# Two of four activation buffers are shifted by 16 and 48 bytes against the 64-byte lines of SBUF

## The chip, the cores and the metric

The kernel runs on one core of a Trainium2 chip. The metric is the device time of one execution in microseconds.

## What is computed

Two transformer blocks one after the other, on 512 tokens of width 1024, in fp32. The first: a mixer (an eight-head forgetting attention and a gated linear attention beside it), a cross-attention over 256 memory tokens, and an MLP of width 4096 with a squared ReLU. The second: a gated MLP of width 2816, a token mixer (a differential attention, and a sparse attention with compressed, selected and windowed keys, merged by two gates), another gated MLP, and a last norm. Nearly all the work is dense products of activations with weight matrices:

```
proj = xn @ w_in
u = jax.nn.relu(rms_norm(h, norm_mlp_g) @ mlp_w1)
h = h + (u * u) @ mlp_w2
return (jax.nn.silu(h @ w1) * (h @ w3)) @ w2
merged = jax.nn.sigmoid(g_a) * (y_da @ w_proj_da) + jax.nn.sigmoid(g_b) * (y_ns @ w_proj_nsa)
```

## The kernel before, in words

A product of two fp32 matrices is made of three matmuls of the type float32r. Each operand is held as a high part and a low part (the high part is a rounded copy, the low part is the operand less the high part), and the helper `product` (L973 to L977) multiplies high by high (L975), high by low (L976) and low by high (L977) into the same PSUM bank. This is called a triple below. The second argument of a matmul in the code is the weights operand (loaded into the array), the third is the moving one (streamed through it); a profile's row names both, in no fixed order.

The activations lie in SBUF in two pairs of buffers, `xh` and `xl` (the pair X) and `ah` and `al` (the pair Y), each of 8 tiles of 128 partitions by 512 tokens, 16,384 bytes a partition. While one stage's input is read from one pair, the next stage's is often written into the other. The weights come as panels of 256 columns into `raw` (SyncE issues these DMAs), ScalarE makes the high part `wh` of a panel and VectorE the low part `wl`, each double buffered.

Four kinds of stage use these buffers:

- `panel_t` (L983): a panel's columns are the weights operand, 128 at a time, and the activations move, 512 columns wide. 2 x 8 triples a panel. This is most of L975 to L977.
- `panel_n` (L998): the activations are the weights operand and the panel's 256 columns move. Used where tokens are to lie on partitions.
- The MLPs' products by a Strassen-like scheme of seven products of half-size blocks (L1530 to L1532 and L1550 to L1552), 256 columns wide. Their operands are blocks of `arena_r`, `wh`, `wl` and, in some of them, of the X and Y buffers.
- Small products of the attentions, out of `arena`.

In the MLP stages the storage of the X and Y buffers that is not in use also takes raw weight blocks: `xh_f`, `xl_f`, `ah_f` and `al_f` are fp32 views of the same bytes as four blocks of 4 x 256 elements, written by DMA and read by ScalarE and VectorE. The low parts are written by VectorE: by a subtraction in `low` (L2817) and by one scalar-tensor-tensor operation (L2830) in `norm_low`.

The buffers are laid out one after another by an allocator that rounds to 32 bytes (L379 to L392). By the built program's addresses `h` begins at byte 2176 of a partition, `xh` at 18560, `xl` at 34944, `ah` at 51328, `al` at 67712, `raw` at 84096, `wh` at 100480, `wl` at 116864 and `cst` at 133248. All of these are multiples of 64. `arena` and `arena_r`, the same bytes, begin 32 bytes past a multiple of 64; blocks in them lie whole multiples of 64 bytes further. Tiles and blocks of the activation buffers, too, are whole multiples of 64 bytes long.

The order of work is written out by hand: each engine has its own list of instructions, with semaphores for what it needs of the others. The change touches no such list.

Of the kernel before, what the change touches and what calls it, by code (L numbers as in the profile page):

```python
# [7 lines left out]
F32 = mybir.dt.float32  # L8
F32R = mybir.dt.float32r
AX = mybir.AxisListType  # L10

PART = 128
T, M, D = 512, 256, 1024
KT = D // PART
PC = 256
QT = T // PART
HALF = 64
D_FF, D_FF2 = 4096, 2816
CMP_L, CMP_S = 32, 16
NCMP = (T - CMP_L) // CMP_S + 1  # L20
# [87 lines left out]
HT = KT // 2  # L108
# [198 lines left out]
def constants():  # L307
# [4 lines left out]
    def put(name, a):  # L312
        nonlocal at
        a = np.asarray(a, np.float32).reshape(PART, -1)
        where[name] = at
        at += a.shape[1]
        parts.append(a)
# [13 lines left out]
    put("cmpany", (valid.any(-1)).astype(np.float32).T)  # L331
    put("tril", (p[:, None] % HALF) <= np.arange(HALF)[None, :])
    put("chunk", np.tile(np.arange(T)[None, :] % HALF != 0, (PART, 1)))
    put("block", (p[:, None] // HALF) == (p[None, :] // HALF))
    inv = (np.float32(1.0) / (np.float32(10000.0) ** (np.arange(0, HALF, 2, dtype=np.float32) / np.float32(HALF)))).astype(np.float32)
    ang = (np.arange(T, dtype=np.float32)[:, None] * inv[None, :]).astype(np.float32)
    put("cos", np.cos(ang).T[p % (HALF // 2)])
    put("sin", np.sin(ang).T[p % (HALF // 2)] * np.where(p % HALF < HALF // 2, -1.0, 1.0)[:, None])
    sel = np.zeros((PART, 4))
# [29 lines left out]
def build(nc, d, out):  # L369
    ctx = ExitStack()  # L370
    with ctx:
        def sb(name, shape, dt=F32):
            return ctx.enter_context(nc.sbuf_tensor(name, shape, dt))
# [7 lines left out]
        xh = sb("xh", [PART, KT, T], F32R)  # L381
        xh_f = nc.alloc_sbuf_tensor_at("xh_f", [PART, 4, HT, PC], F32, offset=xh_at)
        xl_at = -(-nc.sbuf_base // 32) * 32
        xl = sb("xl", [PART, KT, T], F32R)
        xl_f = nc.alloc_sbuf_tensor_at("xl_f", [PART, 4, HT, PC], F32, offset=xl_at)
        ah_at = -(-nc.sbuf_base // 32) * 32
        ah = sb("ah", [PART, KT, T], F32R)
        ah_f = nc.alloc_sbuf_tensor_at("ah_f", [PART, 4, HT, PC], F32, offset=ah_at)
        al_at = -(-nc.sbuf_base // 32) * 32
        al = sb("al", [PART, KT, T], F32R)  # L390
        al_f = nc.alloc_sbuf_tensor_at("al_f", [PART, 4, HT, PC], F32, offset=al_at)
        raw = sb("raw", [PART, 2, KT, PC])  # L392
        wh = sb("wh", [PART, 2, KT, PC], F32R)
        wl = sb("wl", [PART, 2, KT, PC], F32R)
# [3653 lines left out]
```

## Time and profile before

| | |
|---|---|
| median of 3 runs | 2123.26 us (2122.52 to 2123.94) |
| the profiled execution's own time | 2123.62 us |
| its span, first to last instruction | 2121.8 us |
| TensorE busy, matmuls | 2103.8 us (99%), 13292 |
| TensorE busy, weight loads | 1816.3 us (86%) |
| VectorE busy | 1399.6 us (66%) |
| ScalarE busy | 1053.1 us (50%) |
| GpSimd busy | 52.0 us (2%) |

The matmuls overlap: one begins while the one before is still draining, so that the duration of a matmul in a row (390 ns for 512 columns) is longer than the distance from its start to the next one's start. That distance is read from a window, as its length by the number of matmuls that start in it, or from a timeline's column of starts.

### The profile page before, as it was taken

Reading aid. Unit: us, or ns where it says so; the run is one execution under the profiler, and the core shown is the slowest. Engines: PE = TensorE matmul, PEld = TensorE weight load, DVE = VectorE, ACT = ScalarE, POOL = GpSimd, SP = SyncE. Lnnn points to the kernel's source line nnn. Section 1 sums busy time; section 2 is a strip of 40 time slices with the busy share of each in tenths; the row PEclk is TensorE's granted clock in tenths of the full one; section 3 lists DMA queues with packets and bytes.
Section 4 is the critical chain, followed back from the end, with each engine's and each line's share of the span. In section 5 each row is a group of like instructions: output and inputs, shape, how many; then the busy total and the mean of one; then the engine's idle time right before and its main releaser. Section 6 shows DMA issues by size and latency. Waiting matters only on the chain.

```text
span 2121.8 us, 33199 instructions
## 1 busy us (share of the span) xinstructions
PE 2103.8 (99%) x13292; PEld 1816.3 (86%) x13292; DVE 1399.6 (66%) x2337; ACT 1053.1 (50%) x1762; POOL 52.0 (2%) x68
## 2 busy tenths in 40 slices
PE   9999999999999999999999999999999999999999
PEld 7888988888998988899988888887777888899997
DVE  4664663467665767688856777647776357678874
ACT  6664545443533543464543565546667234445454
POOL 0000000000000011110100000000000000000000
PEclk9999999999999999999999999999999999999999
DMA  5121522156355366875543522321111233345432
GB/s 191 60 81 61 192 94 72 40 149 189 102 167 145 94 160 173 229 204 159 142 137 102 179 85 81 99 85 51 27 50 33 88 99 95 104 126 154 129 91 79
DMA packets 210827, 243.83 MB, mean 115 GB/s; under 512 B 9953, under 2 KB 193394, under 8 KB 210162
## 3 DMA queue, kind: packets, MB, share of 16 engines
q1 hardware_dynamic: 199410, 208.15, 31.1%
q0 software_dynamic: 11264, 33.56, 7.4%
q8 instruction: 106, 1.74, 0.3%
q14 instruction: 47, 0.39, 0.1%
HBM read 232.77 MB, written 35.65 MB: 127 GB/s over the span
## 4 chain that ended last, share of the span: by engine, by line
PE 95%; DVE 2%; ACT 1%; issue 1%; DMA 0%; SPq 0%; DVEq 0%; ACTq 0%
PE lin L975 19%; PE lin L977 19%; PE lin L976 19%; PE turned L1076 3%; PE score L1171 3%; PE score L1551 3%; PE score L1552 3%; PE mix L1552 3%; PE mix L1551 3%; PE score L1550 3%; PE mix L1550 3%; PE mix L1185 2%; PE turned L1552 1%; PE turned L1551 1%; PE turned L1550 1%; PE mix L1724 1%
## 5 line engine op out<-in xcount | busy, mean ns | idle before, releaser
L975 PE MATMUL lin<-xh,wh 128*128 128x512 f32 (+1 forms) x968 | 382.5, 395 | 1.7 <-DVE wl L2812 1.2
L977 PE MATMUL lin<-xh,wl 128*128 128x512 f32 (+1 forms) x968 | 369.9, 382 | 0.0
L976 PE MATMUL lin<-xl,wh 128*128 128x512 f32 (+1 forms) x968 | 368.8, 381 | 0.0
L975 PE MATMUL lin<-ah,wh 128*128 128x512 f32 x724 | 283.6, 392 | 1.4 <-DVE al L2817 0.6
L977 PE MATMUL lin<-ah,wl 128*128 128x512 f32 x724 | 281.1, 388 | 0.0
L976 PE MATMUL lin<-al,wh 128*128 128x512 f32 x724 | 280.9, 388 | 0.0
L2806 DVE TENSOR_TENSOR wl<-raw,wh 128x2048 fp32r<-128x2048 f32 x77 | 176.5, 2293 | 117.8 <-ACT wh L1890 117.8
L975 PEld LDWEIGHTS lin<-xh,wh 128*128 128x128 f32 x968 | 182.2, 188 | 43.0 <-issue 9.6
L977 PEld LDWEIGHTS lin<-xh,wl 128*128 128x128 f32 x968 | 182.0, 188 | 36.3
L976 PEld LDWEIGHTS lin<-xl,wh 128*128 128x128 f32 x968 | 182.5, 188 | 32.5 <-issue 1.0
L1890 ACT ACTIVATE wh<-raw 128x2048 fp32r<-128x2048 f32 x77 | 146.8, 1906 | 95.9 <-PE lin L977 80.7
L975 PEld LDWEIGHTS lin<-ah,wh 128*128 128x128 f32 x724 | 136.0, 188 | 30.8 <-issue 1.6
L977 PEld LDWEIGHTS lin<-ah,wl 128*128 128x128 f32 x724 | 135.9, 188 | 28.1
L976 PEld LDWEIGHTS lin<-al,wh 128*128 128x128 f32 x724 | 136.0, 188 | 27.7 <-issue 0.2
L2812 DVE TENSOR_TENSOR wl<-raw,wh 128x1024 fp32r<-128x1024 f32 x90 | 109.5, 1221 | 40.2 <-ACT wh L1897 39.6
L2920 DVE CUSTOM_DVE_ANT_0 arena<-score,cst 128x128 f32<-128x128 f32 (+2 forms) x224 | 97.6, 487 | 57.7 <-PE score L1171 46.6
L1975 ACT ACTIVATE arena<-turned 128x512 f32<-128x512 f32 (+1 forms) x128 | 68.9, 582 | 112.4 <-PE turned L1076 112.1
L1987 ACT ACTIVATE arena<-arena,negm 128x128 f32<-128x128 f32 (+2 forms) x224 | 122.9, 555 | 3.0 <-DVE negm L2920 3.0
L2817 DVE TENSOR_TENSOR wl<-raw,wh 128x1024 fp32r<-128x1024 f32 x84 | 102.3, 1221 | 26.5 <-ACT wh L2435 25.2
L1897 ACT ACTIVATE wh<-raw 128x1024 fp32r<-128x1024 f32 x90 | 94.1, 1053 | 35.5 <-PE lin L977 22.2
L2435 ACT ACTIVATE wh<-raw 128x1024 fp32r<-128x1024 f32 x70 | 73.9, 1056 | 66.6 <-PE score L1552 22.0
L1551 PE MATMUL mix<-arena_r,wh 128*128 128x256 f32 x320 | 89.5, 280 | 0.0
(563 smaller groups left out, 4735.9 us busy)
## 6 DMA issues: line engine op xcount, KB each, us to landing
raw<-in_w_in_dram SPq DMA_DIRECT2D x38, 1024.0 KB, 5.3
raw<-in_ffn_w_dram SPq DMA_DIRECT2D x46, 512.0 KB, 4.3
raw<-in_mlp_w_dram SPq DMA_DIRECT2D x20, 1024.0 KB, 5.6
raw<-in_ffn_w_dram SPq DMA_DIRECT2D x20, 1024.0 KB, 5.3
up_sums_ffn<-in_ffn_w_dram POOLq DMA_DIRECT2D x32, 512.0 KB, 5.4
down_sums_ffn<-in_ffn_w_dram POOLq DMA_DIRECT2D x24, 512.0 KB, 5.9
raw<-in_xattn_wkv_dram SPq DMA_DIRECT2D x8, 1024.0 KB, 5.3
raw<-in_w_out_dram SPq DMA_DIRECT2D x8, 1024.0 KB, 5.2
```

The source lines that it names most:

```text
L975: nc.tensor.matmul(o, w[0], x[0], start=first, stop=False)
L976: nc.tensor.matmul(o, w[0], x[1], start=False, stop=False)
L977: return nc.tensor.matmul(o, w[1], x[0], start=False, stop=last)
L1550: nc.tensor.matmul(o[:, c, :], left_h[:, k, cols], right_h[:, k, :], start=begins, stop=False, skip_group_check=True)
L1551: nc.tensor.matmul(o[:, c, :], left_h[:, k, cols], right_l[:, k, :], start=False, stop=False, skip_group_check=True)
L1552: mm = nc.tensor.matmul(o[:, c, :], left_l[:, k, cols], right_h[:, k, :], start=False, stop=k == HT - 1, skip_group_check=True)
L1890: nc.scalar.activation(wh[:, p % 2], raw[:, p % 2], ACT.Copy).then_inc(hi_done, 1)
L1987: op = nc.scalar.activation(PB[:, s % 2, a, col:col + nk], SM[:, a, col:col + nk], ACT.Exp, bias=negm[:, at:at + 1], scale=-1.0, accum_out ...
L2806: nc.vector.tensor_tensor(wl[:, p % 2], raw[:, p % 2], wh[:, p % 2].bitcast(F32), ALU.subtract).then_inc(conv_done, 1)
L2812: nc.vector.tensor_tensor(wl[:, p % 2, :, cols], raw[:, p % 2, :, cols], wh[:, p % 2, :, cols].bitcast(F32), ALU.subtract).then_inc(conv_d ...
L2817: nc.vector.tensor_tensor(dst, full, hi.bitcast(F32), ALU.subtract).then_inc(done, 1)
L2920: op = nc.vector.tensor_tensor_reduce(out=SM[:, a, col:col + nk], in0=ps[a][:, col:col + nk], in1=mask, scale=scale, scalar=BIG, op0=ALU.a ...
```

## The change

`xl` and `al` each get an allocation longer by 16 elements (64 bytes), and begin 4 elements (16 bytes) and 12 elements (48 bytes) into it. Their fp32 views are made in the same way over the same bytes. With this `xl` begins at 34960 (16 past a multiple of 64), `ah` at 51392, `al` at 67824 (48 past), and all that follows lies 128 bytes further than before. No instruction is added, removed or moved, and none changes but for its addresses.

```diff
+LOW_X, LOW_Y = 4, 12
...
-        xl = sb("xl", [PART, KT, T], F32R)
-        xl_f = nc.alloc_sbuf_tensor_at("xl_f", [PART, 4, HT, PC], F32, offset=xl_at)
+        xl_room = sb("xl", [PART, 16 + KT * T], F32R)
+        xl = xl_room[:, LOW_X:LOW_X + KT * T].rearrange("p (k n) -> p k n", k=KT)
+        xl_f = nc.alloc_sbuf_tensor_at("xl_f", [PART, 16 + KT * T], F32, offset=xl_at)[:, LOW_X:LOW_X + KT * T].rearrange("p (b k n) -> p b k n", b=4, k=HT)
...
-        al = sb("al", [PART, KT, T], F32R)
-        al_f = nc.alloc_sbuf_tensor_at("al_f", [PART, 4, HT, PC], F32, offset=al_at)
+        al_room = sb("al", [PART, 16 + KT * T], F32R)
+        al = al_room[:, LOW_Y:LOW_Y + KT * T].rearrange("p (k n) -> p k n", k=KT)
+        al_f = nc.alloc_sbuf_tensor_at("al_f", [PART, 16 + KT * T], F32, offset=al_at)[:, LOW_Y:LOW_Y + KT * T].rearrange("p (b k n) -> p b k n", b=4, k=HT)
```

## Rows read from the trace of the kernel before

**Rows 1.** Spans by core, and of the page: busy times, and the chain's shares.

```profile
core 0: 2121.8 us, clock 1.000
...
PE 2103.8 (99%) x13292; PEld 1816.3 (86%) x13292; DVE 1399.6 (66%) x2337; ACT 1053.1 (50%) x1762; POOL 52.0 (2%) x68
...
PE 95%; DVE 2%; ACT 1%; issue 1%; DMA 0%; SPq 0%; DVEq 0%; ACTq 0%
```

**Rows 2.** Groups by form, TensorE: matmuls with a low part; busy us, mean ns.

```profile
L976 PE MATMUL lin<-xl,wh 128*128 128x512 f32 x888 | 346.2, 390 | 0.0
...
L976 PE MATMUL lin<-al,wh 128*128 128x512 f32 x716 | 278.7, 389 | 0.0
...
L977 PE MATMUL lin<-wh,xl 128*128 128x256 f32 x256 | 72.3, 283 | 0.0
...
L976 PE MATMUL lin<-xl,wh 128*128 128x256 f32 x80 | 22.6, 283 | 0.0
...
L1551 PE MATMUL score<-al,wh 128*128 128x256 f32 x48 | 13.6, 283 | 0.0
L1551 PE MATMUL score<-xl,wh 128*128 128x256 f32 x48 | 13.6, 283 | 0.0
...
L977 PE MATMUL lin<-wh,xl 128*128 128x512 f32 x32 | 12.4, 389 | 0.0
...
L1551 PE MATMUL mix<-xl,wh 128*128 128x256 f32 x32 | 9.1, 283 | 0.0
L1551 PE MATMUL mix<-al,wh 128*128 128x256 f32 x32 | 9.1, 283 | 0.0
```

**Rows 3.** Windows, TensorE: stretch, us, PE busy (matmuls), clock, DMA share, GB/s.

```profile
653.26:696.80 43.54, 43.54 (x194) 1.00 0.69 198
...
552.74:564.13 11.39, 11.39 (x98) 1.00 0.01 2
967.30:978.81 11.51, 11.51 (x98) 1.00 0.79 256
981.69:993.19 11.50, 11.50 (x98) 1.00 0.34 99
882.37:893.63 11.26, 11.26 (x98) 1.00 0.86 246
924.79:936.05 11.26, 11.26 (x98) 1.00 0.62 148
893.64:896.50 2.86, 2.86 (x26) 1.00 0.72 222
978.82:981.68 2.86, 2.86 (x26) 1.00 0.12 41
```

**Rows 4.** Timeline, TensorE, 512-wide matmuls after a break: start us, us.

```profile
280.49 0.40 PE L976 MATMUL lin<-al,wh 128*128 128x512 f32 x1
280.72 0.40 PE L977 MATMUL lin<-ah,wl 128*128 128x512 f32 x1
...
282.34 0.39 PE L975 MATMUL lin<-ah,wh 128*128 128x512 f32 x1
```

**Rows 5.** Groups by form, VectorE, line 2817; transfers: KB each, us to landing.

```profile
L2817 DVE TENSOR_TENSOR al<-arena,ah 128x512 fp32r<-128x512 f32 x54 | 36.8, 688 | 22.2 <-ACT ah L2371 10.7 <-ACT ah L2495 8.9 <-ACT ah L2444 1.4
...
L2817 DVE TENSOR_TENSOR arena_r<-arena,arena_r 128x512 fp32r<-128x512 f32 x20 | 13.3, 685 | 0.0
...
xl_f<-in_mlp_w_dram SPq DMA_DIRECT2D x12, 512.0 KB, 8.5
...
xl_f<-in_ffn_w_dram SPq DMA_DIRECT2D x6, 512.0 KB, 4.3
```

**Rows 6.** Waits of TensorE, the two longest: us in total, times, longest.

```profile
PE lin L1232 <- DMA gT<-in_gains_dram: 2.6, 1, 2.6
PE turned L1076 <- DVE arena L2936: 1.9, 4, 0.6
```

## The prediction

> **What bounds the kernel now.** I read the page first. TensorE is busy for 2103.8 of 2121.8 us, the granted clock is 1.000 of the 2.4 GHz level from end to end, and 95% of the chain that ended last is TensorE's own work [rows 1]. Its longest wait in the whole span is 2.6 us, before the first matmul; the next is 1.9 us in four pieces [rows 6]. So what counts is the distance from the start of one matmul to the start of the next, and the change can act on that alone: it adds, removes and moves no instruction.
>
> Next I read by form which matmuls touch the low parts [rows 2]. 512 columns wide: 888 with `xl` and 716 with `al` as the moving operand and 32 with `xl` as the weights, 1636 in all. 256 columns wide: 80, 48, 48, 32 and 32 with a low part moving, 256 with `xl` as the weights, and by the program's operands 112 more in smaller groups, 608 in all. Each is one of a triple (high by high, high by low, low by high), so 2244 triples hold one touched matmul, and the two others keep their addresses. Some 40 more have 48 or 64 weight columns; I leave them out.
>
> Then I took windows of uninterrupted matmuls, to read a distance with its addresses [rows 3]. A window counts also the two matmuls in flight at its edges, so 98 stand for 96 starts. By the program's addresses all buffers up to `cst` start on a 64-byte line and `arena` starts 32 bytes past one. I call that offset the phase of an operand.
> - 512 wide, `ah` and `al` with `wh` and `wl`, moving and weights at phase 0 (653.26): 43.54 us / 192 = 226.8 ns.
> - 256 wide, the X and Y buffers with `wh` and `wl`, both at 0 (967.30 and 981.69): 11.51 / 96 = 119.9 ns and 11.50 / 96 = 119.8 ns.
> - 256 wide, `arena_r` with `arena_r`, both at 32 (893.64): 2.86 / 24 = 119.2 ns.
> - 256 wide, `arena_r` moving at 32, weights `wh` and `wl` at 0 (882.37, 924.79): 11.26 / 96 = 117.3 ns; in another stage (552.74) 11.39 / 96 = 118.6 ns.
> - 256 wide, `ah` and `al` moving at 0, weights `arena_r` at 32 (978.82): 2.86 / 24 = 119.2 ns.
>
> So the phase matters in the kernel as it stands: equal phases give 120 ns steadily, unequal ones mostly less, never more. The last thing read is what a 512-wide run does after a break [rows 4]: from 280.49 to 282.34 it makes eight steps in 1.85 us, 231.3 ns each, uneven ones of 0.22 to 0.24 us, and then goes at an even 0.23. The even pace of 226.8 ns is thus something that the stream falls into, and it is the better pace for 512 columns, while for 256 columns the even pace (120) is the worse one. Whether the shifted operand keeps the stream out of that pace is the whole question.
>
> **The change part by part.**
> *High parts, weights, arena.* `ah` moves by 64 bytes and all behind `al` by 128, whole lines: their phases stay, priced at nothing.
>
> *Writers of the low parts.* DVE writes `al` at phase 0 in 688 ns and `arena_r` at phase 32 in 685 ns with the same operation and shape [rows 5], so a shifted output costs nothing; were it 10 ns on each of the some 250 operations, that would be 2.5 us on an engine busy for 66%, beside TensorE, whose largest wait for DVE is 1.9 us in four pieces [rows 6]. Nothing, then.
>
> *Transfers into the low parts.* By the program 21 land in `xl_f` and 9 in `al_f`, 512 KB each, in runs of 1 KB; the two largest groups, 12 and 6 of them, take 8.5 and 4.3 us [rows 5]. With a 16- or 48-byte offset a run touches one more 64-byte line, 17 for 16, an estimated 6% or 0.5 us of 8.5. No matmul waits for these transfers [rows 6], so I price it at nothing; were each of the 30 late by 0.5 us and nothing in between, 15 us would be the bound, and the cover is that SyncE runs buffers ahead.
>
> *Matmuls with a low part.* No row shows a 512-wide matmul at unequal phases. The nearest rows bound it. Below: the 117.3 ns of the unequal 256-wide run against 119.9, a gain of 2.6 ns. Taken for all three of a triple it is 7.8 ns x 2244 = 17.5 us. Above: the uneven pace, 231.3 against 226.8, a loss of 4.5 ns, taken for all three of the 1636 wide triples: 22.1 us. I take one gain of 2.6 ns in each triple, for the one matmul whose phase then differs from its partner's. The row is the nearest in kind (equal against unequal phases in an uninterrupted stream, same data type, same weights), and the loss belongs to a stream just restarted. Wide: 1636 x 2.6 ns = 4.3 us; narrow: 608 x 2.6 ns = 1.6 us. Sum: -5.9 us against the profiled execution's 2123.6 us, 2117.7; that execution stands 0.4 us over the median of the runs shown, so 2117.3 us.
>
> What the rows say of the two reads is that they are tied: the distance at 256 columns depends on the phase of the weights against that of the moving operand (117.3 against 119.2 and 119.9 with the moving operand at 32, 0 and 0). The Trainium skill ("TensorE: Matmul & The Clock Gate", Step-by-step) says otherwise: TensorE has two independent read ports, and loading the next weights takes no read bandwidth from the running matmul; by that rule the sum would be 0 and the time stay. The trace disagrees at 256 columns, by 2.6 ns.
>
> **The rivals.**
> *1. Nothing measurable: the wide stream keeps its pace.* Each start shifts with its operand, the step into the low part is longer by a fraction and the one out of it shorter by the same. For it: runs with both at 0 and both at 32 have the same pace [rows 3]. Against it: the unequal runs differ. Only the narrow triples would gain, at most 1.6 us: 2121.7 us. The Trainium skill ("SBUF — State Buffer", the section on the DMA port swizzle) has a rule that would come out here too: lines are of 16 bytes, and what costs is a crossing between them. Shifts of 16 and 48 bytes leave the number of 16-byte lines as it is, so by it nothing changes. The 32-byte phase of `arena` is a multiple of 16 as well, and its rows differ from phase 0 at 256 columns, so the trace speaks against that rule as a full account.
>
> *2. Slower: the wide stream loses its even pace.* One operand in three off the common phase could keep the 512-wide stream in the uneven steps of [rows 4]. For it: the unequal narrow runs never settle to an even 120, and at 512 columns the uneven pace is the dearer one. Against it: only a third of the operands differ. Price: 4.5 ns on all three matmuls of 1636 triples, +22.1 us, less 1.6 for the narrow ones: 2143.8 us; if only the touched matmul loses 4.5 ns, +7.4 - 1.6: 2129.1 us. It decides from the point where the wide loss exceeds the narrow gain, 1.6 us / 1636 = 1.0 ns a triple, and the kernel is slower by over 0.2% from (4.2 + 1.6) us / 1636 = 3.5 ns a triple.
>
> *3. Faster by more: the whole triple gains.* If the unequal pace spreads to all three, as in the windows in which all are unequal: 2123.3 - 17.5 = 2105.8 us. For it: the two high matmuls follow and precede a shifted one. Against it: their own phases stay equal.
>
> *4. The change doesn't do what it says.* It would have to leave the phases alone. The allocation is rounded to 32 bytes, and the room of 16 elements is a whole line, so the phases of 16 and 48 bytes come out as stated; under 1 in 50, in the share of rival 1.
>
> **How the numbers follow.** Forecast and rival 3 together 0.45 (0.33 and 0.12), rival 1 0.20, rival 2 0.35 (0.15 for the single loss, 0.20 for the whole triple). The likeliest is the forecast, 2117.3 us, and by itself it reaches from 2112 to 2119. Cases of both signs hold most of the chance, so the range reaches from rival 3's 2105 to 2142, just short of the full price of rival 2, which leaves out some 2 in 10. About 0.2%, 4.2 us, is what a measurement of this kernel can tell from no change; so faster 0.45, within 0.2% 0.20, slower 0.35.
>
> **What would show it.** Right: windows of the 512-wide stages (the one of 192 starts took 43.54 us) shorter by 64 x 2.6 ns = 0.17 us, with the starts of L976 no longer evenly spaced; the 256-wide runs of `xh`, `xl`, `ah`, `al` with `wh` under 119.9 ns; durations of L976 differing from L975 and L977. Wrong in the direction of rival 2: the same window at 43.54 + 192 x 4.5 ns = 44.4 us, with steps of 0.22 to 0.24 us all through. Rival 1: 43.54 us again. Wrong altogether: windows without a low part (552.74 of the kernel before, `arena_r` with `wh`) change their length, or TensorE gets waits for DVE or for a transfer into `xl_f` or `al_f`.

## The result, and the profile after

The changed kernel takes 2136.95 us (median of 4 runs, 2136.40 to 2137.29) against 2123.57 us for the kernel before beside it: a ratio of 1.0065, with a 95% interval of 1.0053 to 1.0077. It is slower by 13.4 us. The forecast was 2117.3 us and faster; the measured time lies inside the range, between the two prices of rival 2 (2129.1 and 2143.8).

The span and clock, and of the page the busy times and the chain by engine, against [rows 1]:

```profile
core 0: 2135.3 us, clock 1.000
...
PE 2119.1 (99%) x13292; PEld 1813.2 (85%) x13292; DVE 1399.8 (66%) x2337; ACT 1052.6 (49%) x1762; POOL 51.9 (2%) x68
...
PE 95%; DVE 2%; ACT 1%; issue 1%; DMA 0%; SPq 0%; DVEq 0%; ACTq 0%
```

The counts are equal and the clock still full. The span grew by 13.5 us and TensorE's busy time by 15.3; VectorE, ScalarE and GpSimd stayed within 0.5. So the time is not in a new wait. TensorE's list of waits, in which none grew by more than 0.1 us, confirms that; its two longest, against [rows 6] (columns: total us, times, longest; three lines of code were added, so that L1079 is the L1076 of before, and L978 to L980 are the high-high, high-low and low-high matmuls of a triple):

```profile
PE lin L1235 <- DMA gT<-in_gains_dram: 2.7, 1, 2.7
PE turned L1079 <- DVE arena L2939: 1.9, 4, 0.6
```

The two suspected side costs, the write of `al` by VectorE and the transfers into `xl_f`, against [rows 5]:

```profile
L2820 DVE TENSOR_TENSOR al<-arena,ah 128x512 fp32r<-128x512 f32 x54 | 36.8, 688 | 22.3 <-ACT ah L2374 10.7 <-ACT ah L2498 8.9 <-ACT ah L2447 1.4
...
xl_f<-in_mlp_w_dram SPq DMA_DIRECT2D x12, 512.0 KB, 8.3
xl_f<-in_ffn_w_dram SPq DMA_DIRECT2D x6, 512.0 KB, 4.7
```

688 ns as before, and 8.3 and 4.7 us where it was 8.5 and 4.3: nothing waits on either. What is left is the pace of the matmuls. The same windows as [rows 3], found by their matmuls (the window's length in us, PE busy and matmuls, clock, DMA share, GB/s):

```profile
656.47:701.05 44.58, 44.58 (x195) 1.00 0.68 195
974.15:985.40 11.25, 11.25 (x99) 1.00 0.84 255
889.37:900.63 11.26, 11.26 (x99) 1.00 0.94 267
555.34:566.73 11.39, 11.39 (x99) 1.00 0.01 2
985.39:988.18 2.79, 2.79 (x27) 1.00 0.26 91
```

- The 192 wide matmuls on `ah` and `al` take 44.58 us where they took 43.54: 232.2 ns each, not 226.8.
- The 96 narrow ones on X with `wh` and `wl` take 11.25 us where they took 11.51: 117.2 ns, not 119.9.
- The two windows of `arena_r` with `wh` and `wl` keep 11.26 and 11.39 us, 117.3 and 118.6 ns.
- The 24 with Y moving and arena weights: 2.79 us where it was 2.86, 116.3 ns against 119.2.

All three matmuls of a wide triple grew, not only the one with the low part. The groups by form, first of the kernel before, then of the changed one (the before of `al` is in [rows 2], 389 ns):

```profile
L975 PE MATMUL lin<-ah,wh 128*128 128x512 f32 x716 | 281.1, 393 | 1.4 <-DVE al L2817 0.6 <-DVE h L2867 0.5 <-issue 0.3
L977 PE MATMUL lin<-ah,wl 128*128 128x512 f32 x716 | 278.9, 389 | 0.0
...
L978 PE MATMUL lin<-ah,wh 128*128 128x512 f32 x716 | 284.1, 397 | 1.0 <-DVE h L2870 0.5 <-DVE al L2820 0.5
L979 PE MATMUL lin<-al,wh 128*128 128x512 f32 x716 | 282.6, 395 | 0.0
L980 PE MATMUL lin<-ah,wl 128*128 128x512 f32 x716 | 282.2, 394 | 0.0
```

**Where the 13.4 us lie.** I matched the matmul records of the two traces with the program's operands, took for each the distance to the next one's start, and summed the differences. Wide matmuls with Y moving: +10.7 us. With X moving: +6.4. Narrow ones of the arena against `wh` and `wl`: -0.2. All other classes together: -3.5. In groups of eight consecutive matmuls, those that ran at an even 226.7 ns before (some 1860 with Y moving, 1288 with X; the first count moves by some 50 with where the groups are cut) lost about 10.1 and 5.7 us, 5.4 and 4.4 ns each; the other wide matmuls lost about 1.3 us in all.

### The profile page after: what moved, and what is told of

The parts are those of the page before. It is cut to its first block, busy times and chain, and to the rows that moved or that the text cites. A ratio compares the mean times of both kernels' runs of the same rounds, so it can differ in the third digit from the quotient of the medians.

```text
span 2135.3 us, 33199 instructions
## 1 busy us (share of the span) xinstructions
PE 2119.1 (99%) x13292; PEld 1813.2 (85%) x13292; DVE 1399.8 (66%) x2337; ACT 1052.6 (49%) x1762; POOL 51.9 (2%) x68
## 4 chain that ended last, share of the span: by engine, by line
PE 95%; DVE 2%; ACT 1%; issue 1%; DMA 0%; SPq 0%; DVEq 0%; ACTq 0%
PE lin L978 19%; PE lin L979 19%; PE lin L980 19%; PE turned L1079 3%; PE score L1174 3%; PE score L1555 3%; PE score L1553 3%; PE mix L1555 3%; PE score L1554 3%; PE mix L1554 3%; PE mix L1553 3%; PE mix L1188 2%; PE turned L1555 1%; PE turned L1553 1%; PE turned L1554 1%; PE mix L1727 1%
## 5 line engine op out<-in xcount | busy, mean ns | idle before, releaser
L978 PE MATMUL lin<-xh,wh 128*128 128x512 f32 (+1 forms) x968 | 384.2, 397 | 1.7 <-DVE wl L2815 1.2
L980 PE MATMUL lin<-xh,wl 128*128 128x512 f32 (+1 forms) x968 | 371.3, 384 | 0.0
L978 PE MATMUL lin<-ah,wh 128*128 128x512 f32 x724 | 286.7, 396 | 1.0 <-DVE h L2870 0.5
L980 PE MATMUL lin<-ah,wl 128*128 128x512 f32 x724 | 284.5, 393 | 0.0
L978 PEld LDWEIGHTS lin<-xh,wh 128*128 128x128 f32 x968 | 181.6, 188 | 45.3 <-issue 9.5
L980 PEld LDWEIGHTS lin<-xh,wl 128*128 128x128 f32 x968 | 181.8, 188 | 38.6
L978 PEld LDWEIGHTS lin<-ah,wh 128*128 128x128 f32 x724 | 136.5, 189 | 33.4 <-issue 1.2
L980 PEld LDWEIGHTS lin<-ah,wl 128*128 128x128 f32 x724 | 135.7, 187 | 32.1
L2870 DVE TENSOR_TENSOR h<-lin,h 128x512 f32<-128x512 f32 x56 | 38.6, 689 | 78.9 <-PE lin L980 78.8
```

The costliest lines, as they stand in the source:

```text
L978: nc.tensor.matmul(o, w[0], x[0], start=first, stop=False)
L980: return nc.tensor.matmul(o, w[1], x[0], start=False, stop=last)
```

## The experiments

Fifteen more kernels ran: thirteen forms of the whole kernel and two small tables of streams (e5 and e8). The kernel before took 2123.2 to 2123.5 us beside them. The table gives the differences by class as above, in us, between the profiled executions; "arena" is the class of 2,808 narrow matmuls with `arena_r` moving and `wh` or `wl` as weights. "Displaced" means that the rooms of 64 bytes push `ah` and `al` on by 64 bytes and all behind them by 128. A place is an address modulo 256 bytes: before, X, Y, `wh` and `wl` are all at 128, the arena at 32.

| run | what differs from before | median us | ratio, interval | wide Y | wide X | arena | other |
|---|---|---|---|---|---|---|---|
| after | the change | 2136.95 | 1.0053 to 1.0077 | +10.7 | +6.4 | -0.2 | -3.5 |
| e1 | `xl` shifted 16, displaced | 2138.80 | 1.0057 to 1.0090 | +13.1 | +6.5 | -0.2 | -3.9 |
| e2 | `al` shifted 48, displaced | 2140.57 | 1.0067 to 1.0098 | +10.5 | +10.1 | -0.3 | -3.6 |
| e3 | displaced only | 2142.39 | 1.0077 to 1.0107 | +13.1 | +9.6 | -0.2 | -3.8 |
| e4 | `wh` +16, `wl` +80, arena +128 | 2138.76 | 1.0059 to 1.0089 | +12.8 | +10.7 | -5.0 | -3.1 |
| e6 | displaced by multiples of 256 | 2122.70 | 0.9989 to 1.0008 | 0.0 | +0.1 | 0.0 | -0.8 |
| e7 | both shifts, not displaced | 2146.06 | 1.0094 to 1.0124 | +17.1 | +8.0 | 0.0 | -2.4 |
| e9 | `wh`, `wl` +16 | 2146.69 | 1.0096 to 1.0127 | +10.8 | +6.6 | +6.4 | -2.9 |
| e10 | `wh`, `wl` +16, arena +128 | 2145.01 | 1.0087 to 1.0115 | +11.2 | +10.1 | +4.9 | -4.7 |
| e11 | arena +32 | 2121.54 | 0.9983 to 1.0001 | -0.2 | -0.2 | 0.0 | -1.6 |
| e12 | arena +64 | 2123.97 | 0.9994 to 1.0012 | -0.1 | -0.2 | +1.8 | -0.9 |
| e13 | arena +96 | 2130.25 | 1.0020 to 1.0045 | -0.1 | -0.1 | +6.6 | +0.6 |
| e14 | arena +160 | 2113.73 | 0.9942 to 0.9967 | 0.0 | -0.6 | -8.6 | 0.0 |
| e15 | arena +224 | 2127.49 | 1.0010 to 1.0028 | 0.0 | -0.2 | +3.8 | +0.7 |

Of e9 the profiled execution was the fastest of four, 2144.54 us; they spread to 2148.30, where no other form of the kernel spread over more than 1.4 us.

### One part at a time: e1, e2, e3

```diff
-LOW_X, LOW_Y = 4, 12
+LOW_X, LOW_Y = 4, 0
```

This is e1, against the changed kernel; e2 has `0, 12` and e3 `0, 0`. The rooms of 64 bytes stay, and with them the displacement of `ah` by 64 bytes and of the weights by 128.

> xl 16 bytes past a line, al at 0 with its longer room. Theory A (a 512-wide triple loses its even pace when one of its operands is off the common phase, each pair of buffers by itself): in the run with both shifts the wide triples of the X pair took 693.3 ns against 680, so the 920 of them cost 7 to 12 us less what the narrow ones give back (about 2.5 us): 2128 to 2131 us, and the wide stages on ah and al are back at 226.8 ns a matmul. Theory B (the displacement of what lies behind, or the transfers, makes the loss): near the 2137 us of both shifts, or near 2123.6, but not in between by the counts of triples.

> al 48 bytes past a line, xl at 0 with its longer room. Theory A: the 716 wide triples of the Y pair took about 697 ns against 680 with both shifts, 10 to 12 us, less 1 us or so for the narrow ones: 2132 to 2134 us; the windows on xh and xl are back at 226.8 ns. Together with the run of X alone the two differences should add up to the 13.4 us of both. Theory B as for X alone.

> Both rooms of 16 more elements, both low parts at 0: only the displacement by 64 and 128 bytes is left. Theory A: 2123.6 us within 1 us, 226.8 ns a wide matmul. Theory B (displacement): most of the 13.4 us is still there.

The window of the 192 wide matmuls on Y in e3, where no low part is shifted:

```profile
658.29:703.09 44.80, 44.80 (x195) 1.00 0.68 197
```

44.80 us, 233.3 ns each: worse than with the change (44.58). The rooms alone, with every operand in its old place within a 64-byte line, cost 19.1 us, more than the whole change. In this displaced layout the shifts of 16 and 48 bytes give 5.4 us back (2142.39 against 2136.95), and each on its own buffer: the wide X class goes from +9.6 to +6.5 with the shift of `xl` alone, the wide Y class from +13.1 to +10.5 with that of `al` alone. A whole line of 64 bytes is not a neutral distance. Theory A, which made the low parts alone answerable, fell in all three runs (it had 2128 to 2131, 2132 to 2134 and 2123.6 us); theory B, the displacement, held in e3, and with more than the whole loss.

### The weights moved instead: e4

```diff
-        wh = sb("wh", [PART, 2, KT, PC], F32R)
-        wl = sb("wl", [PART, 2, KT, PC], F32R)
+        wh = sb("wh", [PART, 16 + 2 * KT * PC], F32R)[:, W_AT:W_AT + 2 * KT * PC].rearrange("p (s k n) -> p s k n", s=2, k=KT)
+        wl = sb("wl", [PART, 16 + 2 * KT * PC], F32R)[:, W_AT:W_AT + 2 * KT * PC].rearrange("p (s k n) -> p s k n", s=2, k=KT)
```

with `W_AT = 4`.

> The kernel before with both weight buffers wh and wl 16 bytes past a line, all activations at 0. Theory A1 (what counts in a wide stream is that the moving operands agree among themselves; the weights' load is hidden behind 512 columns): the wide stages stay at 226.8 ns, the narrow ones (0 against 16, and 32 against 16) stay or go down to 117 to 118: 2118 to 2123 us. Theory A2 (what counts is that weights and moving operand agree): all wide triples lose 4 to 5 ns a matmul, 15 to 25 us: 2137 to 2147 us.

```profile
657.26:702.04 44.78, 44.78 (x195) 1.00 0.70 196
890.78:901.90 11.12, 11.12 (x99) 1.00 0.94 270
```

The wide stream loses as before (233.2 ns) though no activation buffer moved: theory A1 fell and A2 held, with 2138.76 us in its 2137 to 2147. What counts is how the operands lie to one another, not where the low part lies in its line. The second row is new: narrow matmuls of the arena at 11.12 us / 96 = 115.8 ns, where they take 117.3.

### Two tables of paces: e5 and e8

Two small kernels run uninterrupted streams of 144 matmuls of the same triple, each with other offsets of high part, low part, `wh` and `wl`.

> No part of the block is computed: only a table of paces. 50 runs of 144 triples' matmuls, each run on a line of its own, with the high and low moving operand and the weights at phases of 0, 16, 32 and 48 bytes, 512 and 256 columns wide, and some with 32 weight columns. Theory A1 (the moving operands must agree with each other): at 512 columns every run with the low part at the phase of the high part is at 226.7 ns a matmul whatever the weights' phase, the others at 229 to 233. Theory A2 (weights against moving): 226.7 only where all three phases are equal. In both a low part 64 bytes off is at 226.7, and equal phases of 16 or 32 are as good as 0. At 256 columns equal phases 120, unequal ones 116 to 119. With 32 weight columns: by a tie between the two reads the loss of the unequal runs shrinks or goes, by a cost of the moving reads alone it stays.

> No part of the block is computed: a table of paces, 53 runs of 144 matmuls, each on a line of its own. High and low moving operand lie 16384 bytes apart and the weights a multiple of 16384 bytes from them, as in the kernel before, and each run then shifts the low moving operand, the weights or both by 16 to 1024 bytes. The first run, without a shift, is at 226.7 ns. Theory D: so is every run whose shifts are multiples of 256, and those with weights 64 or 128 bytes off are at 230 to 235. Theory E: shifts of 256 to 1024 lose the pace too. Theory D1: a low part 16 or 32 bytes off with the weights in place keeps 226.7; theory D2: it doesn't. 256 columns wide: 120 without a shift, 116 to 119 with one.

Each ran once. In e5 the buffers never lay all in one place modulo 256, and nearly all its wide streams ran at 231 to 234 ns, equal places within a line or not, so that both its theories fell; one stream with unequal places (L78 of e5, the offset of the low part 32) took 226.9. That led to 256 bytes, and in e8 the buffers lie 16,384 bytes apart, all at 128 modulo 256 as in the kernel. The timeline of e8 (start, length, line; the distance is the next row's start less this one's, over 144). L73 to L76 have the low moving part 48, 64, 128 and 256 bytes on:

```profile
123.94 34.06 PE L73 MATMUL acc<-mv,wt 128*128 128x512 f32 x144
157.84 33.57 PE L74 MATMUL acc<-mv,wt 128*128 128x512 f32 x144
191.25 33.44 PE L75 MATMUL acc<-mv,wt 128*128 128x512 f32 x144
224.53 32.81 PE L76 MATMUL acc<-mv,wt 128*128 128x512 f32 x144
257.18 32.80 PE L77 MATMUL acc<-mv,wt 128*128 128x512 f32 x144
```

235.4, 232.0, 231.1 and 226.7 ns. L79 to L81 have both weights 16, 32 and 64 bytes on, L92 to L94 all four operands 16, 64 and 128 bytes on together, and L96 to L99 the layouts of four stages of the kernels (read further down):

```profile
322.46 32.81 PE L79 MATMUL acc<-mv,wt 128*128 128x512 f32 x144
355.11 33.75 PE L80 MATMUL acc<-mv,wt 128*128 128x512 f32 x144
388.70 33.76 PE L81 MATMUL acc<-mv,wt 128*128 128x512 f32 x144
422.30 33.88 PE L82 MATMUL acc<-mv,wt 128*128 128x512 f32 x144
...
753.76 33.44 PE L92 MATMUL acc<-mv,wt 128*128 128x512 f32 x144
787.04 32.85 PE L93 MATMUL acc<-mv,wt 128*128 128x512 f32 x144
819.72 32.85 PE L94 MATMUL acc<-mv,wt 128*128 128x512 f32 x144
852.41 32.81 PE L95 MATMUL acc<-mv,wt 128*128 128x512 f32 x144
885.06 33.45 PE L96 MATMUL acc<-mv,wt 128*128 128x512 f32 x144
918.35 33.60 PE L97 MATMUL acc<-mv,wt 128*128 128x512 f32 x144
951.79 33.76 PE L98 MATMUL acc<-mv,wt 128*128 128x512 f32 x144
985.39 33.75 PE L99 MATMUL acc<-mv,wt 128*128 128x512 f32 x144
1018.98 33.92 PE L100 MATMUL acc<-mv,wt 128*128 128x512 f32 x144
```

226.7, 233.3 and 233.3 ns; then 231.1, 226.9 and 227.0; and for L96 to L99 231.2, 232.2, 233.3 and 233.3. Shifts of 256, 512 and 1024 bytes, of the low part or of the weights, all gave 226.7: theory D held, E fell, and of the two on shifts within a line D2 held. The very first stream, without a shift, took 238.8 ns in the mean and not the 226.7 expected, because its first eight steps took 0.38 to 0.59 us; the same layout ended at 226.7 there and had 226.7 again as L95. No wide stream of the table went faster than that, and all but one of those with unequal places took 229 to 235. The exception is L79, the weights 16 bytes on. The other way round, L92, with all four in one place but 16 bytes past a multiple of 64, had 231.1, so one common place is not enough by itself.

Narrow streams differ. L110 has all in one place, L118 the weights 64 bytes on:

```profile
1351.71 17.44 PE L110 MATMUL acc<-mv,wt 128*128 128x256 f32 x144
1368.98 17.28 PE L111 MATMUL acc<-mv,wt 128*128 128x256 f32 x144
...
1488.18 16.49 PE L118 MATMUL acc<-mv,wt 128*128 128x256 f32 x144
1504.51 17.24 PE L119 MATMUL acc<-mv,wt 128*128 128x256 f32 x144
```

119.9 ns (17.27 us / 144) and 113.4 (16.33 us / 144); the others between 116.7 and 120.0.

### Modulo 256 in the kernel: e6 and e7

```diff
-LOW_X, LOW_Y = 4, 12
+LOW_X, LOW_Y, ROOM = 0, 0, 64
...
-        xl_room = sb("xl", [PART, 16 + KT * T], F32R)
+        xl_room = sb("xl", [PART, ROOM + KT * T], F32R)
...
-        al_room = sb("al", [PART, 16 + KT * T], F32R)
+        al_room = sb("al", [PART, ROOM + KT * T], F32R)
```

against the changed kernel; e7 has `LOW_X, LOW_Y, ROOM = 4, 12, 64`.

> Both rooms longer by 64 elements in place of 16 and both low parts at 0, so that ah begins 256 bytes later and everything behind al 512 bytes later: every buffer keeps its place modulo 256. The runs so far showed that the displacement alone (64 and 128 bytes) costs more than the change. Theory D (the pace of a wide stream hangs on where weights and activations lie against each other within 256 bytes): all wide stages back at 226.8 ns a matmul, 2123 to 2124.5 us. Theory E (it hangs on more address bits, up to 16384 bytes, or on what else moved): still 2135 to 2145 us.

> The change's shifts of 16 and 48 bytes in rooms longer by 64 elements: the phases of the change, without its displacement modulo 256. Theory D1 (only the displacement cost anything, and a shift by less than a line is harmless or good): 2116 to 2124 us. Theory D2 (a shift within a line breaks the even pace as well, by itself): wide triples at 693 ns as with the change, 2133 to 2145 us.

e6, then e7, each with the wide window on Y:

```profile
652.43:695.97 43.54, 43.54 (x194) 1.00 0.67 194
```

```profile
659.78:704.99 45.21, 45.21 (x195) 1.00 0.69 196
```

e6 is the kernel before to 0.1%, class by class: with rooms of 256 bytes the displacement costs nothing, with rooms of 64 it costs 19.1 us. So the place modulo 256 decides, shown in the kernel itself: theory D held and E fell. e7 gives the shifts alone: they break the even pace without any displacement (235.5 ns in the window) and cost 22.8 us, more than in the layout of the change. D1 fell; D2 had the direction, 1.1 us short of the time. The two causes do not add: each ends the even pace, and what follows is the pace of the layout that they make together.

That pace stands in e8. By the built programs' addresses both kernels and table have their buffers at 128 modulo 256, so a layout can be named by how far high part, low part, `wh` and `wl` lie past that. The kernel's figure is the mean over the wide matmuls that ran at 226.7 ns before:

| layout (bytes) | row of e8, ns | in the kernel, ns |
|---|---|---|
| 64, 112, 128, 128 | L97, 232.2 | Y with the change 232.1, in e2 232.1 |
| 0, 16, 128, 128 | L96, 231.2 | X with the change 231.1, in e1 231.1 |
| 64, 64, 128, 128 | L98, 233.3 | Y in e1 233.3, in e3 233.3 |
| 0, 0, 128, 128 | L83, 232.3 | X in e2 232.9, in e3 232.5 |
| 0, 0, 16, 80 | L99, 233.3 | X and Y in e4 233.3 |
| 0, 48, 0, 0 | L73, 235.4 | Y in e7 235.4 |
| 0, 16, 0, 0 | L71, 232.1 | X in e7 232.0 |

Twelve means, eleven of them within 0.2 ns of a stream that computes nothing and has no other engine at work beside it. So the loss of the change is the pace of its own layout: it needs no wait, no transfer and no neighbour to explain it.

### The weights on 16 bytes, twice: e9 and e10

```diff
-        wh = sb("wh", [PART, 2, KT, PC], F32R)
-        wl = sb("wl", [PART, 2, KT, PC], F32R)
+        wh = sb("wh", [PART, 64 + 2 * KT * PC], F32R)[:, 4:4 + 2 * KT * PC].rearrange("p (s k n) -> p s k n", s=2, k=KT)
+        wl = sb("wl", [PART, 64 + 2 * KT * PC], F32R)[:, 4:4 + 2 * KT * PC].rearrange("p (s k n) -> p s k n", s=2, k=KT)
```

(e10: 32 in place of 64 for `wl`.)

> Both weight buffers begin 16 bytes past a 64-byte line, with room of 256 bytes behind each, so that wh and wl stay 16,384 + 256 bytes apart and cst and the arena lie 512 bytes further, in their old places modulo 256. No activation buffer moves. Theory F (the paces of the table of runs carry over into the kernel): the wide triples, whose moving parts lie in equal places, keep 226.7 ns a matmul, as the table's row with the weights 16 bytes on, and the narrow ones may gain up to 1.6 ns, as the table has 118.3 against 119.9: 2117 to 2123 us. Theory G (any shift between moving operand and weights that is no multiple of 64 breaks the even pace): the wide classes lose 2.5 to 5 ns a matmul, 2135 to 2146 us.

> As the run with both weight buffers on 16 bytes, but with room of 128 bytes behind wl, so that the arena lies 384 bytes further: 128 on modulo 256, and 16 bytes from the place of the weights, as it lay to wh in the run with wh on 16 bytes alone, where the narrow triples out of the arena gained 5.0 us. Theory F: wide unchanged and the narrow triples of the arena against wh and wl at 115.9 ns where they take 117.7: 2116 to 2119 us, faster than before. Theory G: slower, 2132 to 2142 us.

Theory F fell in both: the one unequal layout that kept 226.7 ns in the table (L79) costs +17.4 us over the wide classes in e9. But it did not go everywhere. In e9, a stage on X, one on Y and another on Y:

```profile
791.95:835.47 43.52, 43.52 (x194) 1.00 0.63 163
852.69:874.45 21.76, 21.76 (x97) 1.00 0.82 231
658.19:680.59 22.40, 22.40 (x97) 1.00 0.56 162
```

43.52 us / 192 and 21.76 us / 96 are both 226.7 ns; 22.40 us / 96 is 233.3. Of the 399 groups of eight that ran at the even pace before, 96 keep it in e9, and all the others run at 233.3 ns; in e10, with the same places of X, Y, `wh` and `wl`, 28 keep it. So this layout has two paces, and a stream goes on in one of them until its next break. L79 came without a pause behind three streams at the even pace; whether that set its own was not tested. A single row of the table can thus show one pace of two.

Theory G had the direction; its range was 0.7 us short for e9 and 3 us short for e10, because the arena class, expected to keep still or gain, lost 6.4 and 4.9 us. In e10 the arena lies to `wh` as it did in e4, where the class gained 5.0 us; what differs is `wl`, 64 bytes off `wh` in e4 and equal to it here.

### Only the arena moved: e11 to e15

```diff
+        sb("gap", [PART, 8])
         arena_at = -(-nc.sbuf_base // 32) * 32
```

8 elements in e11; 16, 24, 40 and 56 in e12 to e15.

> Only the arena moves, by 32 bytes, onto a multiple of 64. The wide triples, whose operands are all in X, Y, wh and wl, stay as they are (0.0 us). The narrow ones, some 3700 matmuls with an arena operand, take another pace: between 113.4 and 120 ns where they take 117.7, by the spread of the table's 256-wide runs, so -16 to +8 us; if the gain of 5.0 us in the run with wh on 16 bytes came of wh and wl lying unequal, nothing: 2123.2 us.

> Only the arena moves, by 64 bytes; its place within a line stays, its place modulo 256 changes. Wide triples 0.0 us. If the place modulo 256 between moving operand and weights counts for narrow triples as it does for wide ones, the classes with an arena operand change their pace by 0.5 to 4 ns, -14 to +8 us in all; if only the relation between the two parts of an operand counts, nothing: 2123.2 us.

> Only the arena moves, by 96 bytes, to 128 modulo 256, where the other buffers lie: every operand of every float32r product now lies in one place modulo 256. Theory H (one place for all is even for narrow products too, and evenness there is the slow pace, 120 ns, as the table has 119.9): the 2,808 narrow matmuls of the arena against wh and wl go from 117.7 to about 120 ns, +6.5 us, the 360 against xh from 118.7 to 120, +0.5 us: about 2130 us. Rival (the place counts for wide products alone): 2123 us.

> Only the arena moves, by 160 bytes, to 192 modulo 256, 64 bytes from the place of the others. The 144 matmuls with the arena as weights and X or Y moving take 113.4 ns where they take 119.4 (-0.9 us), by the table's row with the weights 64 bytes on. The 2,808 with the arena moving: 113.4 ns and -12 us if the distance of 64 bytes alone sets the pace whichever operand is ahead (2110 us); 117.7 to 118.6 ns, as in the run with the arena on 32 bytes, if it does not (2122 to 2125 us).

> Only the arena moves, by 224 bytes, to 0 modulo 256, 128 bytes from the place of the others. The table has 116.7 ns with the low moving part 128 bytes on and 118.6 with the weights 128 bytes on, against 119.9: the 2,808 narrow matmuls out of the arena between 116.7 and 118.6 ns, -3 to +3 us: 2120 to 2126 us.

The wide classes moved by at most 0.6 us in any of them. e11 and e12 are not clear of noise in their times (both intervals include 1), and there only the classes are read: e12 keeps the arena's place within a line of 64, and its class still goes from 117.7 to 118.3 ns. e15 missed: 2127.49 us where at most 2126 was expected, because the class ran at 119.0 ns in the mean and not at up to 118.6. The two windows of the arena class, in e13 and in e14:

```profile
883.19:894.71 11.52, 11.52 (x99) 1.00 0.92 258
552.49:564.01 11.52, 11.52 (x99) 1.00 0.01 2
```

```profile
881.27:892.15 10.88, 10.88 (x99) 1.00 0.99 275
552.34:563.65 11.31, 11.31 (x99) 1.00 0.01 2
```

With the arena in the place of all the others (e13) both windows take 120.0 ns, and the class +6.6 us where +6.5 was expected: for narrow products the even pace of one common place is the slow one. 64 bytes further than the others (e14) they take 113.3 and 117.8 ns, the class gains 8.6 us of the 12 that a full 113.4 would give, and the kernel runs in 2113.73 us, faster than before by 9.5 us and than the change by 23. The 144 matmuls with arena weights, expected to gain 0.9 us, gained under 0.3.

In e11 it was those 144 that gained, 119.4 to 113.3 ns, as this window of 24 shows (2.72 us / 24 = 113.3), while the arena class went to 117.8 in both windows:

```profile
880.54:891.85 11.31, 11.31 (x99) 1.00 0.95 261
977.12:979.84 2.72, 2.72 (x27) 1.00 0.05 18
```

In both cases of 113.3 ns the moving operand and the weights are 64 bytes apart with the weights at the lower place (e11: weights at 64, moving at 128; e14: weights at 128, moving at 192). The mirror cases, weights at the higher place, gave 117.8 in both runs, but 113.4 in the table. And e14's second window has the layout of its first and 117.8 ns: a layout can have two paces for narrow products as well. The rival of e14, that the distance alone decides, is thus neither confirmed in full nor fallen. The first window of the class by the arena's place: 117.3 at 32, 117.8 at 64, 118.3 at 96, 120.0 at 128, 113.3 at 192, 118.6 ns at 0.

## Why the prediction was wrong

**What bounds the kernel** held: what changed is the distance between matmuls. No wait of TensorE grew by more than 0.1 us, the write of `al` kept its 688 ns, and the two groups of transfers into `xl_f` moved by 0.4 us at most.

**"High parts, weights, arena", priced at nothing because whole lines keep the phases.** This step failed. The phase was taken modulo 64, on lines of 64 bytes that no run shows, and e3 charges 19.1 us for the displacement that this step calls neutral, while e6 charges nothing for one by multiples of 256. In [rows 3] all wide operands lie in one place modulo 64 and modulo 256 alike, and the rows could not tell the two apart. The rows of `ah` moving with arena weights (119.2 ns at unequal phases, as much as `arena_r` with `arena_r` at equal ones) were a hint that the 64-byte phase didn't explain the narrow paces either.

**"Matmuls with a low part": a gain of 2.6 ns per triple.** This step failed too, in its sign for the wide ones. It priced a wide matmul off the common place by a narrow row. The other row stood beside it, the uneven steps of [rows 4], and the prediction itself called the even pace the better one for 512 columns; it then let the nearer kind of row decide between the two. With no displacement (e7) the same shifts cost 25.1 us in the wide classes, where -4.3 had been written. The narrow term had the right sign: -1.6 us written, -3.5 measured over all narrow and small classes, and the window of X with `wh` went from 119.9 to 117.2 ns, a gain of 2.7 where 2.6 was taken. It came also in matmuls with no operand in a shifted buffer (the 360 of `arena_r` with `xh` weights: 118.7 to 116.8). The narrow classes with an operand in X or Y gained 3.5 us with the change, 3.5 with the displacement alone (e3) and 2.4 with the shifts alone (e7), so in the changed kernel the displacement, which the term left out, suffices for the gain: the right sign is partly luck.

**Rival 2** had half of the mechanism: the wide stream loses its even pace, in all three matmuls of a triple. Its cause, one operand in three off the common phase, is a sufficient one (e7: 2146.06 us, against its 2143.8), but in the changed kernel the displacement alone does more (e3), and the shifts give some of it back. That its window comes out so close, 44.4 us and 231.3 ns forecast against 44.58 and 232.2, is therefore partly luck. It priced 1636 triples at 13.5 ns, 22.1 us. Measured were 17.1: some 3150 matmuls, not 4908, had the even pace to lose, and lost 5.0 ns each (15.8 us), the rest 1.3. The chance of 0.35 was too low: its argument against, that only a third of the operands differ, is refuted by e7, where only the low parts lie elsewhere and the even matmuls of Y went from 226.7 ns to 233.3, 238.1 and 234.9 for high by high, high by low and low by high.

**Rivals 1 and 3** fell: the wide stream neither kept its pace nor gained. Rival 1 had leaned on a rule of the Trainium skill ("SBUF — State Buffer", on the DMA port swizzle: lines of 16 bytes, the cost at a crossing). The offsets of 64 and 128 bytes in e3 and e8 leave every crossing of such a line as it was, and the wide pace went from 226.7 to between 228.9 and 234.4 ns: by the trace that rule is not the whole account. The trace disagrees with the Trainium skill, "TensorE: Matmul & The Clock Gate" (Step-by-step), by which the weight load takes no read bandwidth from the running matmul, so far as that would make the place of the weights indifferent: moving only the weights changed the pace of the stream, by 6.6, 6.6 and 5.6 ns in e8 at 32, 64 and 128 bytes (L80, L81 and L83 against 226.7).

**The sign "wrong altogether"** named windows without a low part, and those it named (`arena_r` with `wh`) kept 11.26 and 11.39 us. They lie in a class whose operands were all displaced by 128 bytes together. The sign was well chosen for a wait and blind to a displacement. The matmuls of `arena_r` with `xh` as weights would have been the ones to name: they hold no shifted operand, and went from 118.7 to 116.8 ns.

**What stays open** is what happens in the chip every 256 bytes. The runs show that the pace depends on the places of moving operand and weights to one another, not by what they are joined. Also open: what puts a stream in one or the other pace where a layout has two (226.7 and 233.3 ns in e9, 113.3 and 117.8 in e14), and why four operands in one place lose the even pace 16 bytes past a multiple of 64 (L92) and keep it at 64 and 128.

## What to carry to other kernels

Where TensorE's stream has no gaps, the byte address of a buffer is a parameter like any other: two rooms of 64 bytes between buffers cost 0.9% here, and a gap of 160 bytes before one buffer gained 0.45%. In float32r streams keep the moving parts and the weights of 512-column products in one place modulo 256 bytes, itself a multiple of 64 (L92 to L94), and look for unequal ones for 256-column products. A small stream kernel with the same addresses gave the wide pace of seven layouts to 0.6 ns; measure the layout in the kernel itself all the same, since an eighth had two paces. After any edit to an allocation, read the addresses of all that lies behind it before any other explanation of a few per mille.

## What the runs showed of the hardware

- Wide float32r streams (512 columns) have an even pace of 226.7 ns and several uneven ones from 229 to 236 ns, each belonging to a layout modulo 256 bytes and the same in a bare stream and in the kernel. Every stage kept the even one only with high part, low part, `wh` and `wl` in one place; with both weights 16 bytes on (e9, e10) some stages kept it and others ran at 233.3.
- Narrow streams (256 columns) in one common place take 119.9 to 120.0 ns; other places gave 113.3 to 120.0, and one layout 113.3 in one stage and 117.8 in another.
- The granted clock was 0.999 or 1.000 in every form of the kernel, and TensorE's waits behind its first matmul summed to 7.3 to 10.1 us without following the time, so neither is where such a difference shows. It shows in the length of a window over its matmuls.
